# Moving the norms' coefficient and shift to VectorE and the low-part subtraction to GpSimd

## The reference

```python
def rmsnorm(x, g):
    xf = x.astype(jnp.float32)
    y = xf * lax.rsqrt(jnp.mean(xf * xf, axis=-1, keepdims=True) + EPS)
    return (y * g.astype(jnp.float32)).astype(x.dtype)

def modulate(h, shift, scale):
    return h * (1 + scale) + shift

# in each layer, for the latent and the context tokens, each with its own shift and scale
h = modulate(rmsnorm(x, g_norm1[layer]), sh1, sc1)      # then the token mixer, first product h @ w_in
x = x + gt1 * out
h = modulate(rmsnorm(x, g_norm2[layer]), sh2, sc2)      # then a SwiGLU (layer 0) or 8 experts, top 2 (layer 1)
x = x + gt2 * y
# at the end
return rmsnorm(x, g_final)
```

## Time and profile before

| | |
|---|---|
| median of three runs | 2098.72 us |
| the profiled execution | 2097.66 us |
| its span in the profile | 2095.9 us |
| mean granted clock of TensorE | 0.979 |
| TensorE matmul busy | 2010.5 us (96%) |
| VectorE busy | 1364.4 us (65%) |
| ScalarE busy | 1002.8 us (48%) |
| GpSimd busy | 91.0 us (4%) |
| chain that ended last | TensorE 91%, ScalarE 3%, VectorE 3%, issue 2% |

### The profile page before, as it was taken

One profiled execution on the slowest core, in us unless ns is written; L12 is line 12 of the kernel. 1 busy time (PEld: TensorE's weight loads), 2 busy tenths in 40 slices (PEclk: granted clock), 3 DMA queues, 4 the chain that ended last, 5 costly groups with the idle time before them and its releaser, 6 DMA issues.

```text
span 2095.9 us, 25052 instructions
## 1 busy us (share of the span) xinstructions
PE 2010.5 (96%) x9358; PEld 1585.1 (76%) x9358; DVE 1364.4 (65%) x1588; ACT 1002.8 (48%) x1102; POOL 91.0 (4%) x127
## 2 busy tenths in 40 slices
PE   6999999999899999988999989999999999999995
PEld 3785666667788888868778978887888788878884
DVE  5653343376667556344344468888898889888984
ACT  3423323322522122243433366767676767677774
POOL 0050000010001011003000000000000000000000
PEclk9999999999999999989999979999999999999997
DMA  9412111244255556412233288998998889888960
GB/s 356 141 50 81 51 61 61 111 171 160 86 176 201 181 187 226 151 62 109 81 141 121 91 322 345 350 346 320 343 351 325 341 324 359 335 331 336 358 230 22
DMA packets 72115, 439.85 MB, mean 210 GB/s; under 512 B 9153, under 2 KB 9921, under 8 KB 27457
## 3 DMA queue, kind: packets, MB, share of 16 engines
q1 hardware_dynamic: 60336, 395.23, 49.8%
q0 software_dynamic: 11664, 43.00, 6.0%
HBM read 437.14 MB, written 1.05 MB: 209 GB/s over the span
## 4 chain that ended last, share of the span: by engine, by line
PE 91%; ACT 3%; DVE 3%; issue 2%; DMA 0%; SPq 0%; DVEq 0%; ACTq 0%
PE ps L1490 12%; PE ps L1492 12%; PE ps L1491 12%; PE ps L1855 7%; PE ps L1856 7%; PE ps L1857 7%; PE ps L1704 6%; PE ps L1869 4%; PE ps L1873 4%; PE ps L1870 4%; PE ps L1655 2%; PE ps L1679 2%; PE ps L1525 2%; PE ps L1822 1%; PE ps L1618 1%
## 5 line engine op out<-in xcount | busy, mean ns | idle before, releaser
L1323 DVE TENSOR_TENSOR elo<-estage,ehi 128x2048 fp32r<-128x2048 f32 x267 | 611.7, 2291 | 86.3 <-ACT ehi L876 84.6
L876 ACT ACTIVATE ehi<-estage 128x2048 fp32r<-128x2048 f32 x267 | 510.9, 1914 | 48.3 <-PE ps L1873 48.2
L1490 PE MATMUL ps<-h_hi,whi 128*128 128x512 f32 (+1 forms) x960 | 366.8, 382 | 17.6 <-DVE h_lo L980 8.8
L1491 PE MATMUL ps<-h_lo,whi 128*128 128x512 f32 (+1 forms) x960 | 347.1, 362 | 0.0
L1492 PE MATMUL ps<-h_hi,wlo 128*128 128x512 f32 (+1 forms) x960 | 346.8, 361 | 0.0
L1855 PE MATMUL ps<-ehi,xg_hi 128*128 128x512 f32 x704 | 287.6, 408 | 9.5 <-issue 9.5
L1856 PE MATMUL ps<-elo,xg_hi 128*128 128x512 f32 x704 | 278.6, 396 | 0.0
L1857 PE MATMUL ps<-ehi,xg_lo 128*128 128x512 f32 x704 | 278.0, 395 | 0.0
L957 DVE TENSOR_TENSOR wlo<-stage,whi 128x2048 fp32r<-128x2048 f32 x79 | 181.2, 2295 | 102.1 <-ACT whi L634 102.0
L1490 PEld LDWEIGHTS ps<-h_hi,whi 128*128 128x128 f32 x960 | 183.5, 191 | 67.7 <-issue 29.4
L634 ACT ACTIVATE whi<-stage 128x2048 fp32r<-128x2048 f32 x79 | 150.7, 1909 | 166.5 <-PE ps L1492 166.4
(11 more groups left out here) (212 smaller groups left out, 2495.3 us busy)
## 6 DMA issues: line engine op xcount, KB each, us to landing
estage<-in_moe SPq DMA_DIRECT2D x265, 1024.0 KB, 5.2
stage<-in_split SPq DMA_DIRECT2D x79, 1024.0 KB, 5.0
gw<-in_mods POOLq DMA_DIRECT2D x80, 512.0 KB, 3.8
dw<-in_direct SPq DMA_DIRECT2D x36, 512.0 KB, 3.9
mw_b<-in_mods SPq DMA_DIRECT2D x8, 512.0 KB, 13.0
mw_a<-in_early SPq DMA_DIRECT2D x8, 512.0 KB, 14.5
xT<-in_x SPq DMA_DIRECT2D x1, 2048.0 KB, 8.4
gw<-in_cond_rows SPq DMA_DIRECT2D x1, 1024.0 KB, 5.0
```

The costliest lines, as they stand in the source:

```text
L876: act.activation(ehi[:, w % SPLIT, :], estage[:, w % STAGE, :], ACT.Copy).then_inc(S("e_hi_done"), 1)
L1323: dve.tensor_tensor(elo[:, w % SPLIT, :], estage[:, w % STAGE, :], ehi[:, w % SPLIT, :], ALU.subtract)\
L1490: pe.matmul(out, hi, rhs_hi, start=first, stop=False)
L1491: pe.matmul(out, hi, rhs_lo, start=False, stop=False)
```

## The change

VectorE now makes `nt` and `hf` of a norm: one `tensor_scalar` with two per-partition scalars for each 256 tokens. ScalarE only rounds `hf` to `h_hi`. GpSimd makes `h_lo`. `nt` has three slots in place of two; VectorE issues `nt[k + 1]` ahead of `hf[k]`. In GpSimd's program the subtractions of a norm stand among the loads of the modulation tiles. `pool_in` and one junk tile move by 2048 bytes per partition to make room for the third slot.

```diff
-    pool_in_at = mixer.at + 96
+    pool_in_at = mixer.at + 96 + T * 4
-    nt = nr.take("nt", [P, 2, T])
+    nt = nr.take("nt", [P, 3, T])
-        "in": Region(br_at + 2 * KB * T * 4).take("junk_in", [P, D]),
+        "in": Region(br_at + 2 * KB * T * 4 + T * 4).take("junk_in", [P, D]),
@@ ScalarE, norm
-                    act.activation(o_fin[:, k, :], nt[:, k % 2, 0:n], ACT.Copy,
+                    act.activation(o_fin[:, k, :], nt[:, k % 3, 0:n], ACT.Copy,
...
-            act.wait_ge(S("norm_coef"), 2 * nth(tag) + 2)
-            for k in range(KD):
-                act.wait_ge(S("norm_nt"), KD * nth(tag) + k + 1)
-                if k >= slots:
-                    act.wait_ge(S("norm_hlo"), KD * nth(tag) + k - slots + 1)
-                for s, at in parts:
-                    act.activation(hslot(k, n)[:, at:at + SEQ], nt[:, k % 2, at:at + SEQ], ACT.Identity,
-                                   bias=mod[...], scale=coef[...]).then_inc(S("norm_hf"), 1)
-                if k >= 1:
-                    hi(k - 1)
-            hi(KD - 1)
+            parts = 2 if first == 0 else 1
+            for k in range(KD):
+                act.wait_ge(S("norm_hf"), 2 * KD * nth(tag) + parts * (k + 1))
                 act.activation(h_hi[:, k, first:T], hslot(k, n), ACT.Copy).then_inc(S("norm_hhi"), 1)
@@ VectorE, norm
-            def lo(k):
-                dve.wait_ge(S("norm_hhi"), KD * nth(tag) + k + 1)
-                dve.tensor_tensor(h_lo[:, k, first:T], hslot(k, n), h_hi[:, k, first:T], ALU.subtract)\
-                    .then_inc(S("norm_hlo"), 1)
...
+            def normed(k):
+                if k >= 3 and tag != "fin":
+                    dve.wait_ge(S("norm_hf"), 2 * KD * nth(tag) + (2 if first == 0 else 1) * (k - 2))
+                dve.tensor_tensor(nt[:, k % 3, 0:n], xT[:, k, first:T], ps[6][:, 0:n], ALU.mult).then_inc(S("norm_nt"), 1)
...
+            dve.wait_ge(S("norm_coef"), 2 * nth(tag) + 2)
+            normed(0)
+            for k in range(KD):
+                if k + 1 < KD:
+                    normed(k + 1)
+                dve.wait_ge(S("norm_nt"), KD * nth(tag) + k + 1)
+                if k >= slots:
+                    dve.wait_ge(S("norm_hlo"), KD * nth(tag) + k - slots + 1)
+                for s in (0, 1):
+                    at = s * SEQ - first
+                    if at < 0:
+                        continue
+                    dve.tensor_scalar(hslot(k, n)[:, at:at + SEQ], nt[:, k % 3, at:at + SEQ], coef[:, 2 * layer + i, s, k:k + 1],
+                                      mod[:, layer, s, 3 * i * KD + k:3 * i * KD + k + 1], ALU.mult, ALU.add).then_inc(S("norm_hf"), 1)
@@ GpSimd
+        def norm_lo(tag, first):
+            for k in range(KD):
+                pool.wait_ge(S("norm_hhi"), KD * nth(tag) + k + 1)
+                pool.tensor_tensor(h_lo[:, k, first:T], hslot(k, T - first), h_hi[:, k, first:T], ALU.subtract).then_inc(S("norm_hlo"), 1)
...
+        before_ffn = flush_units(2) - START_UNITS + 2
...
-                load_mods(0, before_windows)
+                load_mods(0, 2)
+                norm_lo("n1_0", 0)
+                load_mods(2, before_windows)
...
-                load_mods(before_windows, len(MOD_TILES) - START_UNITS)
+                load_mods(before_windows, before_ffn)
+                norm_lo("n2_0", 0)
+                load_mods(before_ffn, len(MOD_TILES) - START_UNITS)
+                norm_lo("n1_1", 0)
+            else:
+                norm_lo("n2_1", SEQ)
```

More of the change, by code:

```diff
@@ L663, in norm @@
                     act.wait_ge(S("norm_nt"), KD * nth("fin") + k + 1)
-                    act.activation(o_fin[:, k, :], nt[:, k % 2, 0:n], ACT.Copy,
+                    act.activation(o_fin[:, k, :], nt[:, k % 3, 0:n], ACT.Copy,
                                    scale=gains[:, 2 * DEPTH, k:k + 1]).then_inc(S("out_ready"), 1)
                 return
[L667 to L673, removed]
-                act.activation(h_hi[:, k, first:T], hslot(k, n), ACT.Copy).then_inc(S("norm_hhi"), 1)
-            act.wait_ge(S("norm_coef"), 2 * nth(tag) + 2)
-            for k in range(KD):
-                act.wait_ge(S("norm_nt"), KD * nth(tag) + k + 1)
-                if k >= slots:
-                    act.wait_ge(S("norm_hlo"), KD * nth(tag) + k - slots + 1)
-                for s, at in parts:
-                    act.activation(hslot(k, n)[:, at:at + SEQ], nt[:, k % 2, at:at + SEQ], ACT.Identity,
-                                   bias=mod[:, layer, s, 3 * i * KD + k:3 * i * KD + k + 1],
-                                   scale=coef[:, 2 * layer + i, s, k:k + 1]).then_inc(S("norm_hf"), 1)
-                if k >= 1:
-                    hi(k - 1)
-            hi(KD - 1)
+            parts = 2 if first == 0 else 1
+            for k in range(KD):
+                act.wait_ge(S("norm_hf"), 2 * KD * nth(tag) + parts * (k + 1))
+                act.activation(h_hi[:, k, first:T], hslot(k, n), ACT.Copy).then_inc(S("norm_hhi"), 1)
         act.wait_ge(S("cond_in"), 16)
@@ L976, in norm @@
             dve.wait_ge(S("norm_all"), nth(tag) + 1)
-            def lo(k):
-                dve.wait_ge(S("norm_hhi"), KD * nth(tag) + k + 1)
-                dve.tensor_tensor(h_lo[:, k, first:T], hslot(k, n), h_hi[:, k, first:T], ALU.subtract)\
-                    .then_inc(S("norm_hlo"), 1)
-            parts = 2 if first == 0 else 1
-            for k in range(KD):
[L985 to L996, removed]
+            def normed(k):
+                if k >= 3 and tag != "fin":
+                    dve.wait_ge(S("norm_hf"), 2 * KD * nth(tag) + (2 if first == 0 else 1) * (k - 2))
+                dve.tensor_tensor(nt[:, k % 3, 0:n], xT[:, k, first:T], ps[6][:, 0:n], ALU.mult).then_inc(S("norm_nt"), 1)
+            if tag == "fin":
+                for k in range(KD):
+                    if k >= 3:
+                        dve.wait_ge(S("out_ready"), k - 2)
+                    normed(k)
+                return
+            i = int(tag[1]) - 1
+            layer = int(tag[3])
+            slots = KD * SEQ // n
+            dve.wait_ge(S("norm_coef"), 2 * nth(tag) + 2)
+            normed(0)
+            for k in range(KD):
+                if k + 1 < KD:
[9 more added lines that the diff above has]
+                                      mod[:, layer, s, 3 * i * KD + k:3 * i * KD + k + 1], ALU.mult, ALU.add).then_inc(S("norm_hf"), 1)
         def coefs(layer, i):
```

## The result

| | kernel before | changed kernel |
|---|---|---|
| median of the runs, us | 2101.43 (2096.43 to 2105.65) | 2115.99 (2114.57 to 2117.04) |
| ratio, with its 95% interval | | 1.0072 [1.0059, 1.0086] |
| profiled execution / its span, us | 2097.66 / 2095.9 | 2117.03 / 2115.2 |

The change costs some 14.6 us. I had predicted 2101.6, which is 2.9 us slower, and a range to 2108.0: the direction came out, the size is five times what I had, and the time lies outside the range. The rival called "slower by splitting" had 2113. Of all the executions in this document one is left out of its kernel's ratio: with `nt` in PSUM and the wait, one took 2541.39 us at a granted clock of 0.746, where the ten others took 2099.23 to 2103.25 at 0.976 to 0.979.

The account below looks back on a forecast made before the run. TensorE's waits were taken to bound the kernel. Terms 2.0 (n1_0) + 0.7 (n2_0) + 0.2 (n1_1) gave +2.9 us on 2097.66, so 2100.6; with the median 1.06 above, 2101.6; range 2096.5 to 2108.

Parts of the forecast that it names:

- slower by splitting: Wide norms: GpSimd gets the port between the two `hf` halves, 2.2 us a tile, together +14, 2113 us; chance 12%.
- What bounds the kernel: Whole kernel: TensorE is busy 2010.5 of 2095.9 us, so only what makes it wait can move the end.
- Prices: Per wide tile: GpSimd's subtraction 1.27 us, VectorE's pair of `hf` halves 0.62, up to 0.74.
- Start of the norm: Wide norms: first subtraction runs from offset 2.82 to 4.09 us, so TensorE's start is kept; gain 0.1 left out.
- Exclusion of a single-input `tensor_scalar` and GpSimd: Norms: VectorE's fast single-input form also excludes GpSimd, each waiting for the other's instruction less a 0.14 us head start.
- side by side: Norms: the `tensor_scalar` doesn't exclude GpSimd; TensorE starts 0.25 us earlier in three norms, -0.8, 2097.9; chance 15%.
- VectorE's two `wlo` back to back let nothing in between: Trace row at 976.9, where GpSimd didn't get in; with `hf` pairs uncut, a tile was put at 1.61 to 1.73 us.
- n2_0 and n1_1: Two wide norms: later last `h_hi` delays `whi` and `wlo`; +0.7 us (+0.3 to +1.1) and +0.2 (0 to +0.4).
- n1_0: First wide norm: `wlo` holds GpSimd off with one or two subtractions left; +2.0 us taken, +1.7 to +2.3.
- a case that I had put at +3.5: End of n1_0: the 1.22 us multiply behind `wlo` also slips in ahead of GpSimd; about +3.5 us.
- fin: Last norm: gets only a third `nt` slot, and ScalarE's eight outputs already run gapless; 0 us.
- The range: Whole kernel: from 2096.5 (side by side with a margin) to 2108 us (subtraction of about 1.55); splitting stays outside.

Follow-up runs that it names:

- `nt` in PSUM and the wait: Changed kernel with `nt` of the four split norms in PSUM and VectorE waiting for the last `h_lo` before `wlo`: 2101.25 us, ratio 0.9999.

## Why the prediction was wrong

- **What bounds the kernel**: right. TensorE's waits in and behind the wide norms, and its clock after one of them, make up the 14.2 us; the narrow norm kept its router matmuls at 6.99.
- **Prices**: right. `h_lo` 1.26 to 1.33 (taken: 1.27), a pair of halves 0.73 (taken: 0.62, up to 0.74), the head start of about 0.14 (a pair ended 0.15 behind its `h_lo`), `h_lo` of 256 columns at 0.72 to 0.78 (taken: 0.76).
- **Start of the norm**: right. The first matmul comes at offset 4.02 to 4.07, where it was 4.15 to 4.20 (predicted: kept, gain 0.1 left out).
- **Exclusion of a single-input `tensor_scalar` and GpSimd**: right, as the rule of the Trainium skill (SBUF — State Buffer, "SBUF: two separate sides") had it. `hf` takes 0.90 beside a subtraction and 0.54 alone; with `nt` in PSUM there is none. The rival "side by side" is out.
- **The step that failed**: "VectorE's two `wlo` back to back let nothing in between", carried over to the two halves, and so 1.61 to 1.73 a tile. GpSimd entered at the boundary in every tile where an `nt` stood between two pairs: 2.21. One row of 2048-column instructions was set against another of the same trace where GpSimd had got in behind a multiply, and I gave the second only 12%. The rival's 2.2 came out to 0.01. Its sum was not the cause, though, as the run with two `nt` in a row shows (the same items, 1.74 a tile): it added `nt`, half, subtraction and half, while the loop goes over ScalarE (half b, `h_hi`, `h_lo`) and `nt` only has to be long enough to hold half b back.
- **n2_0 and n1_1**: taken +0.7 and +0.2, measured +2.8 and +2.5. The rival had +5.0 and +4.3. It was too much because for the last two tiles there is no `nt` left: their four halves ran together in 2.33, the last two subtractions behind one another. GpSimd, then VectorE, n2_0, changed kernel; they answer to the earlier trace rows:

```profile
567.36 2.53 POOL L1423 TENSOR_TENSOR h_lo<-hf,h_hi 128x512 fp32r<-128x512 f32 x2 [0.90 <-ACT h_hi L670]
```

```profile
569.76 2.29 DVE L939 TENSOR_TENSOR wlo<-stage,whi 128x2048 fp32r<-128x2048 f32 x1 [2.50 <-ACT whi L634]
```

`wlo` ends at 572.05, offset 20.61 from 551.44, not 22.3.
- **n1_0**: taken +2.0, measured +8.9. Of this 3.1 is the pace. The multiply slipped in too (66.33, 1.21, undisturbed), a case that I had put at +3.5. What I left out is that TensorE came out of the idle time of 3.58 on its lower clock: an estimated 2.7 of the 5.8 us of the intrusion. I had named a low clock only as something that would make the prediction wrong, and gave it no price.
- **fin**: taken 0, because I read ScalarE's eight outputs as gapless. They took 3.89 us, of which 3.6 were busy, and take 3.30 with the third slot; the stretch to the span's end is 8.05, before 8.65. A gain of 0.6 missed, too small for the medians to tell.
- **The range**: it reached only to cases built on the pair that is never cut. With two rows that spoke against each other, the cut pair belonged inside it.

## What to carry to other kernels

Where two engines exclude each other instruction by instruction, don't sum their work: draw the loop of who waits for whom, and look at every boundary between two instructions of one engine where a third engine needs the results of both. One longer instruction, two tiles' worth behind one another, or an input in PSUM took most or all of the loss away here. And when an instruction leaves a queue, look at what now follows the last one left: `wlo` ran ahead and held up the very subtractions that TensorE waited for.

## What the runs showed of the hardware

- The exclusion is of `tensor_scalar` with SBUF input and output as well: 256 columns take 0.41 alone and 1.37 when they have to wait for a subtraction of 1.32. With the input in PSUM they take 0.54 and run beside GpSimd undisturbed, and the subtraction too (1.29).
- GpSimd doesn't always get in at the next boundary. It asked 0.18 after `wlo` began (64.31), let the boundary to the multiply at 66.4 pass and came in at the next (the multiply 1.21, the one behind it 2.27); so too with `nt` in pairs, and with `nt` in PSUM, where its record even starts 0.06 ahead of `wlo`'s (60.40 and 60.46). But where `wlo` had itself waited for a subtraction, the boundary behind it was taken (3.39, then 2.31). Two halves of `hf` behind an `nt` were cut every time that GpSimd asked during the first, 18 times in the changed kernel's wide norms. What decides it stays open: no run varied it alone.
- TensorE's clock in n1_0: after idle times of 3.58 (changed kernel) and 3.21 (`nt` in pairs) there are stretches at 1.2 GHz, with a granted clock from 60 to 80 us of 0.83 and 0.91; with 1.77 and then 0.56 (`nt` in PSUM), and with four of 0.30 to 0.57 (only the subtraction moved), it is 1.00.
